# Taking the low part of five weight slabs from an adding transfer, on one Trainium2 core

## The chip, the cores and the metric

The kernel runs on one core of one Trainium2 chip. The metric is the device time of one execution in microseconds. The kernel before took 734.05 us, the median of three runs (733.32 to 734.15). All times inside the execution come from one profiled execution.

## What is computed

The reference is two blocks of a small transformer-like model on 256 tokens of width 1024, one after the other. The first block is a gated recurrent layer and an attention layer. The second block is a mixer and a feed-forward layer, then a pooling mixer and another feed-forward layer. The stretch around the change is the mixer of the second block:

```python
h = rmsnorm(x, norm_mix_g)
p = h @ w_in_ab                                   # 1024 -> 1536
ya = fnet_heads(p[..., :512], fnet_map)           # Fourier transform over tokens and channels, then a map
u = p[..., 512:1024] * sigmoid(p[..., 1024:])
u = conv31(u) + conv_b                            # a filter of 31 taps along the tokens, per channel
yb = silu(layernorm_per_head(u))
x = x + concat([ya, yb]) @ w_out_ab               # slabs 26 to 29
h = rmsnorm(x, norm_ffn_g)
x = x + (silu(h @ w_gate) * (h @ w_up)) @ w_down  # slabs 30, 31, 32, ...
```

## The kernel before

**Slabs.** The weights stream from HBM in slabs of 128 partitions by 2048 floats (1 MB). SyncE's queue loads each slab into one of five `raw` buffers (L597); before it loads a buffer again it waits until the slab in it has been used. There are 97 slabs that are multiplied in the split form below, numbered 0 to 96 (the list `MATS`).

**The split.** A product in the short float format (fp32r) loses bits, so each weight is written as a high and a low part, and each product is done three times: high by high, high by low and low by high (L1601, L1602 and L1603). Slab k has the tile `W[(k + 2) % 4]`, with the high part in `[:, 0]` and the low part in `[:, 1]`. ScalarE makes the high part, a copy of the raw slab into fp32r (the helper at L629, called in its `stream`), and counts it in `s_hi`. VectorE makes the low part, raw minus high (the helper at L1029, called in its own `stream`), and counts it in `s_lo`. TensorE waits for `s_lo` in `weights(k)`. SyncE frees the raw buffer on `s_lo` as well. ScalarE may overwrite a tile W only when TensorE has finished slab k - 4 (`before_split`).

**The order of work** is written out by hand, on each engine for itself. `fill(k)` on ScalarE and on VectorE splits all slabs up to k + 3 that are not yet split. So the place of a `fill` in an engine's list decides when a slab is split there. The calls that matter here are:

- `fill(24)` splits slabs 26 and 27, `fill(25)` slab 28, `fill(26)` slab 29, `fill(27)` slab 30, `fill(28)` slab 31.
- On ScalarE `fill(24)` stands before the copies of the outputs `a` 0 and 1 (to F2), and `fill(25)` before those of `a` 2 and 3. The products of L1872 read these copies. `fill(26)` stands between the root (L905) and the silu (L911) of the layer norm of head 3. `fill(27)` and `fill(28)` stand before two copies of the mixer's output into X, its squares (L943), and the high parts of the turned X (`turned_high`, L949).
- On VectorE `fill(24)` stands after 36 taps of the convolution (L1032), `fill(25)` after the low parts of the Fourier branch, `fill(26)` after the last taps, and `fill(27)` and `fill(28)` before the low parts of the turned X (`turned_low`, L1032).

Three of the four heads of the convolution are done on VectorE, one multiply-add of 128x256 per tap. Head 3 is done on TensorE (L1894), against diagonal matrices that ScalarE makes.

**TensorE** goes through: the products of slabs 22 to 25; the Fourier products (L1872, L1880, L1881, L1887); the convolution of head 3 (L1894); the residual (L1937); the products of slabs 26 to 29 (the function `mixed`), with the sums of the layer norm between them (L1900, L1905, L1661); then, in the feed-forward layer, turning X (L1927) and `gate_up`, which begins with slab 30. `mixed(7, 1)` is the first that needs slab 29, `mixed(7, 0)` the first that needs slab 28.

**GpSimd's queue** holds only four transfers: the Fourier matrix, then (after `s_flo` reaches 4) the matrix `rc` of the pooling and the row `prow`, then (after `s_cv3`) the row `frow`. `s_flo` counts the low parts of the Fourier branch, which VectorE makes.

Of the kernel before, what the change touches and what calls it, by code (L numbers as in the profile page):

```python
# [93 lines left out]
NRAW, NSPL, LOOK, NT, NB, NSQ = 5, 4, 3, 8, 8, 2  # L94
# [4 lines left out]
MATS = [i for i in RING if PLAN[i][0] not in ("first", "mod")]  # L99
# [11 lines left out]
def width(i):  # L111
    return PLAN[i][4] * 256 if PLAN[i][0] == "mat" else D if PLAN[i][0] == "u" else 2048
# [197 lines left out]

OUT = outputs()

ROWS_AT = {0: 1, 1: 2}
HALF_AT = {k: n + 1 for n, k in enumerate(k for k in range(len(MATS)) if OUT.end[k] is None)}

# [13 lines left out]
def two_block_program(nc, w_d, vec_d, cst_d, dft_d, rcnt_d, row_d, x_d, out_d):  # L329
# [3 lines left out]
    ADD, SUB, MUL = ALU.add, ALU.subtract, ALU.mult  # L333

    ctx = ExitStack()
    with ctx:
        def sb(name, shape, dt=f32):
            return ctx.enter_context(nc.sbuf_tensor(name, shape, dt))

        def sem(name):  # L340
            return ctx.enter_context(nc.semaphore(name))
# [7 lines left out]
        W = [sb(f"w{i}", [P, 2, 2048], f32r) for i in range(NSPL)]  # L349
# [36 lines left out]
            sem(f"s_{n}") for n in ("vec", "id", "xa", "xb", "cst", "dft", "rc", "prow", "frow", "out"))  # L386


        s_hi, s_lo, s_mod, s_half = (sem(f"s_{n}") for n in ("hi", "lo", "mod", "half"))

        s_ps = sem("s_ps")

# [30 lines left out]
        def V(name, i, n=1):  # L423
            return vec[:, VOFF[name] + i:VOFF[name] + i + n]
# [34 lines left out]
        def own_of(slab):  # L459
            return slab[0], slab[1] if slab[0] == "heads" else slab[3]  # L460

        def own(kind, at):

            n = next(n for n, i in enumerate(OWN) if own_of(PLAN[i]) == (kind, at))
            return own_at[kind, at], (s_own[n], 16)
# [4 lines left out]
        def out_of(*name):  # L470
            return PB[OUT.bank[name]][:, 0:T]
# [4 lines left out]
        def quarter(of, a, c):  # L476
            return of[:, a, c * 512:c * 512 + 512]
# [23 lines left out]
        def ended(*name):  # L501
            return s_ps, OUT.count[name]
# [4 lines left out]
        def landed(i):  # L507
            n = RING.index(i)
            return s_raw[n % NRAW], 16 * (n // NRAW + 1)

        def raw_of(i):
            return raw[RING.index(i) % NRAW]

        def before_split(k):

            return slab_ended(k - NSPL) if k >= NSPL else ended(*(("g", 3), ("g", 7), ("y", 3), ("y", 7))[k])
# [6 lines left out]
        def freed(name):  # L523
# [7 lines left out]
            if kind == "n":  # L531
                return s_rt, ROWS_AT[i]
            if kind == "ns":
# [43 lines left out]
        @block.sync  # L577
        def _(e):
            p = Port(e)
            e.dma_start(vec[:, :], vec_d).then_inc(s_vec, 16)  # L580
            e.dma_start(cst[:, 0:P], cst_d[:, 0:P]).then_inc(s_id, 16)
            e.dma_start(X[:, 0:4, :], x_d[:, 0:4, :]).then_inc(s_xa, 16)
            e.dma_start(X[:, 4:8, :], x_d[:, 4:8, :]).then_inc(s_xb, 16)
            n_mod = n_mat = 0
            emptied = []
            for i, slab in enumerate(PLAN):
                n = width(i)
                if i in OWN:
                    if slab[0] == "y":
                        p.wait_ge(*ended("u", 7))  # L590
                    place, done = own(*own_of(slab))
                    e.dma_start(place, w_d[i, :, 0:n]).then_inc(done[0], 16)
                    continue
                m = len(emptied)
                if m >= NRAW:
                    p.wait_ge(*emptied[m - NRAW])
                e.dma_start(raw[m % NRAW][:, 0:n], w_d[i, :, 0:n]).then_inc(s_raw[m % NRAW], 16)  # L597
                if slab[0] in ("first", "mod"):
                    n_mod += 1
                    emptied.append((s_mod, n_mod))  # L600
                else:
                    n_mat += 1
                    emptied.append((s_lo, n_mat))
                    if n_mat == 6:
                        e.dma_start(cst[:, P:NC], cst_d[:, P:NC]).then_inc(s_cst, 16)
            for a in range(2):
                p.wait_ge(s_fin0, a + 1)
                e.dma_start(out_d[:, a, 0:512], quarter(Of, a, 0)).then_inc(s_out, 16)
                p.wait_ge(s_fin1, a + 1)
                e.dma_start(out_d[:, a, 512:1024], quarter(Of, a, 1)).then_inc(s_out, 16)  # L610
            e.wait_ge(s_out, 16 * 4)

        @block.gpsimd
        def _(e):
            e.wait_ge(s_mv, 12)
            e.dma_start(acc[0][:, :], dft_d).then_inc(s_dft, 16)
            e.wait_ge(s_flo, 4)
            e.dma_start(rc, rcnt_d).then_inc(s_rc, 16)
            e.dma_start(prow[:, :], row_d[0]).then_inc(s_prow, 16)
            e.wait_ge(s_cv3, 1)  # L620
            e.dma_start(frow[:, :], row_d[1]).then_inc(s_frow, 16)

        @block.scalar
        def _(e):
            p = Port(e)
            at = {"plan": 0, "mat": 0}

            def copy(out, in_, **kw):
                return e.activation(out, in_, ACT.Copy, **kw)  # L629

            def stream(upto):

                while at["plan"] <= upto:
                    i = at["plan"]
                    at["plan"] += 1
                    if i not in MATS:
                        continue
                    k, n = at["mat"], width(i)
                    at["mat"] += 1
                    p.wait_ge(*landed(i))  # L640
                    p.wait_ge(*before_split(k))
                    copy(W[(k + 2) % NSPL][:, 0, 0:n], raw_of(i)[:, 0:n]).then_inc(s_hi, 1)

            def fill(k):
                stream(MATS[min(k + LOOK, len(MATS) - 1)])
# [18 lines left out]
            def row_root(i):  # L664
                p.wait_ge(*ended("n", i))
                if ROWS_AT[i] > 1:
                    p.wait_ge(s_rs, ROWS_AT[i] - 1)
                e.activation(root[:, :], out_of("n", i), ACT.Sqrt, scale=1.0 / D, bias=V("eps", 0)).then_inc(s_rt, 1)
# [44 lines left out]
            for q in range(2):  # L713
                half = F0f[:, 4 * q:4 * q + 4, :]
# [309 lines left out]
        def _(e):  # L1024
            p = Port(e)
            at = {"plan": 0, "mat": 0, "mod": 0, "vec": 1}

            def tt_(out, a, b, op):
                return e.tensor_tensor(out, a, b, op)  # L1029
# [11 lines left out]
            def mod_sum(i):  # L1041

                m, j = at["mod"], PLAN[i][4]
                u = UNIT_OF[PLAN[i][1:4]]
                at["mod"] += 1
                p.wait_ge(*landed(i))
                p.wait_ge(s_silu, 2)
                for q in range(2):
                    w, total = raw_of(i)[:, q * D:q * D + D], mv[:, u, 2 * j + q:2 * j + q + 1]
                    done = stt(w, w, 1.0, silu_c, MUL, MUL, accum_out=total)  # L1050
                done.then_inc(s_mod, 1)
                bias, off, name, goff = UNITS[u]
                if u in (5, 6):
                    two = mv[:, u, 2 * j:2 * j + 2]
                    p.wait_ge(s_mod, 8 + m + 1)
                    tt_(two, two, V(bias, off + 2 * j, 2), ADD).then_inc(s_mg if name else s_mq, 1)
                    if name:
                        p.wait_ge(s_mg, j + 1)
                        stt(two, two, 1.0, V(name, goff + 2 * j, 2), ADD, MUL).then_inc(s_mq, 1)
                elif j == 3:  # L1060
                    p.wait_ge(s_mod, 8 + m + 1)
                    tt_(mv[:, u, :], mv[:, u, :], V(bias, off, 8), ADD).then_inc(s_gain if name else s_mv, 1)
                    if name:
                        gain(u)

            def stream(upto):

                while at["plan"] <= upto:
                    i = at["plan"]
                    at["plan"] += 1  # L1070
                    if PLAN[i][0] == "mod":
                        mod_sum(i)
                    if i not in MATS:
                        continue
                    k, n = at["mat"], width(i)
                    at["mat"] += 1
                    w = W[(k + 2) % NSPL]
                    p.wait_ge(s_hi, k + 1)
                    tt_(w[:, 1, 0:n], raw_of(i)[:, 0:n], w[:, 0, 0:n].bitcast(f32), SUB).then_inc(s_lo, 1)
# [20 lines left out]
            def row_close(i):  # L1100
                p.wait_ge(s_rt, ROWS_AT[i])
                e.reciprocal(RS[i][:, :], root[:, :]).then_inc(s_rs, 1)
# [63 lines left out]
            z, y_, s_, s2, po = (sm[:, i, :] for i in (1, 3, 4, 5, 6))  # L1166
# [23 lines left out]
            for c in range(4):  # L1190
                for j in range(3):
                    for b in range(2):
                        d, n = 2 * c + b, 6 * c + 2 * j + b
# [398 lines left out]
        def _(e):  # L1592
            p = Port(e)
# [9 lines left out]
                return e.matmul(out, a_lo, b_hi, start=False, stop=stop)  # L1603

            def weights(k):
                p.wait_ge(s_lo, k + 1)

            def tile_of(k, half, o, R, r, out, start, stop, tok):
                w = W[(k + 2) % NSPL]
# [558 lines left out]
```

## Time and profile before

| | |
|---|---|
| median of the runs (lowest, highest) | 734.05 us (733.32, 734.15) |
| span of the profiled execution, first to last instruction | 731.6 us |
| TensorE, products | 719.8 us, 98% of the span |
| TensorE, weight loads | 629.7 us, 86% |
| VectorE | 502.8 us, 69% |
| ScalarE | 395.2 us, 54% |
| GpSimd | 2.4 us |
| mean traffic of the transfers | 213 GB/s |

The profiled execution's own time is not listed beside its span; the median of the runs is 2.45 us above the span. An engine's share says how much of the span it worked, not whether the end waited for it: products on TensorE overlap, and their ends are modelled. The timeline rows have the start in us, the time in us, the engine, the line and the operation, the tile written and the tiles read, the shapes, the count, and in brackets the idle time before it with what ended it.

### The profile page before, as it was taken

Reading aid. Unit: us, or ns where it says so; the run is one execution under the profiler, and the core shown is the slowest. Engines: PE = TensorE matmul, PEld = TensorE weight load, DVE = VectorE, ACT = ScalarE, POOL = GpSimd, SP = SyncE. Lnnn points to the kernel's source line nnn. Section 1 sums busy time; section 2 is a strip of 40 time slices with the busy share of each in tenths; the row PEclk is TensorE's granted clock in tenths of the full one; section 3 lists DMA queues with packets and bytes.
Section 4 is the critical chain, followed back from the end, with each engine's and each line's share of the span. In section 5 each row is a group of like instructions: output and inputs, shape, how many; then the busy total and the mean of one; then the engine's idle time right before and its main releaser. Section 6 shows DMA issues by size and latency. Waiting matters only on the chain.

```text
span 731.6 us, 9776 instructions
## 1 busy us (share of the span) xinstructions
PE 719.8 (98%) x3940; PEld 629.7 (86%) x3940; DVE 502.8 (69%) x801; ACT 395.2 (54%) x614; POOL 2.4 (0%) x8
## 2 busy tenths in 40 slices
PE   7999999999999999999999999999999999999996
PEld 6888889999999999888888888888888888888885
DVE  5879996998877889977744555555686445555544
ACT  3167446874886675658644434443666444344423
POOL 0000000000000000000000000000000000000000
PEclk9999999999999999999999999999999999999999
DMA  8999994798835343423755545554336555455201
GB/s 329 416 422 422 421 410 154 259 396 327 325 124 212 135 161 116 179 102 116 288 177 197 201 173 180 206 190 172 116 116 229 176 198 200 173 181 207 73 1 57
DMA packets 23085, 156.13 MB, mean 213 GB/s; under 512 B 2560, under 2 KB 2816, under 8 KB 5120
## 3 DMA queue, kind: packets, MB, share of 16 engines
q1 hardware_dynamic: 22464, 152.88, 55.2%
q0 software_dynamic: 576, 2.62, 0.9%
q8 instruction: 31, 0.51, 0.3%
q14 instruction: 14, 0.11, 0.0%
HBM read 154.44 MB, written 1.05 MB: 213 GB/s over the span
## 4 chain that ended last, share of the span: by engine, by line
PE 87%; DVE 6%; DMA 4%; ACT 2%; SPq 1%; issue 0%; ACTq 0%
PE pb L1601 22%; PE pb L1603 22%; PE pb L1602 21%; PE pb L1665 10%; DMA raw<-w_dram 4%; DVE raw L1032 3%; DVE w L1029 2%; PE pb L1894 2%; PE pb L2005 1%; PE pb L1758 1%; PE pb L1757 1%; PE pb L1759 1%; PE pb L2073 1%; PE pb L1927 1%; PE pb L1937 0%; PE pb L1872 0%
## 5 line engine op out<-in xcount | busy, mean ns | idle before, releaser
L1029 DVE TENSOR_TENSOR w<-raw,w 128x2048 fp32r<-128x2048 f32 x97 | 221.4, 2291 | 141.2 <-ACT w L629 141.2
L629 ACT ACTIVATE w<-raw 128x2048 fp32r<-128x2048 f32 x97 | 184.9, 1915 | 138.7 <-PE pb L1603 114.7
L1601 PE MATMUL pb<-w,r 128*128 128x512 f32 (+1 forms) x640 | 244.6, 382 | 0.0
L1603 PE MATMUL pb<-w,r 128*128 128x512 f32 (+1 forms) x640 | 241.1, 377 | 0.0
L1602 PE MATMUL pb<-w,r 128*128 128x512 f32 (+1 forms) x640 | 240.7, 376 | 0.0
L1603 PEld LDWEIGHTS pb<-w,r 128*128 128x128 f32 x640 | 120.4, 188 | 22.6
L1601 PEld LDWEIGHTS pb<-w,r 128*128 128x128 f32 x640 | 120.6, 188 | 21.2 <-issue 0.2
L1602 PEld LDWEIGHTS pb<-w,r 128*128 128x128 f32 x640 | 120.6, 188 | 21.0
L1601 PE MATMUL pb<-r,w 128*128 128x256 f32 x288 | 82.5, 287 | 0.4 <-DVE r L1029 0.4
L1603 PE MATMUL pb<-r,w 128*128 128x256 f32 x288 | 81.5, 283 | 0.0
L1602 PE MATMUL pb<-r,w 128*128 128x256 f32 x288 | 81.5, 283 | 0.0
L1032 DVE SCALAR_TENSOR_TENSOR raw<-raw,acc 128x1024 f32<-128x1024 f32 x64 | 75.1, 1221 | 5.0 <-DMA raw<-w_dram 5.0
L1665 PE MATMUL pb<-h,ow 128*128 128x256 f32 x256 | 57.0, 381 | 1.4 <-issue 0.6
L1665 PEld LDWEIGHTS pb<-h,ow 128*128 128x128 f32 x256 | 48.1, 190 | 10.1 <-issue 3.9
L1601 PEld LDWEIGHTS pb<-r,w 128*128 128x128 f32 x288 | 55.2, 192 | 0.6 <-issue 0.6
L1602 PEld LDWEIGHTS pb<-r,w 128*128 128x128 f32 x288 | 55.2, 192 | 0.1
L1603 PEld LDWEIGHTS pb<-r,w 128*128 128x128 f32 x288 | 55.2, 192 | 0.0
L963 ACT ACTIVATE t<-pb,rn 128x256 f32<-128x256 f32 x44 | 20.7, 476 | 59.6 <-PE pb L1603 59.6
L1032 DVE SCALAR_TENSOR_TENSOR f<-f,vec 128x256 f32<-128x256 f32 x114 | 46.7, 482 | 0.2
L1032 DVE SCALAR_TENSOR_TENSOR t<-pb,rn,t 128x256 f32<-128x256 f32 x44 | 21.1, 483 | 22.7 <-ACT t L963 22.7
L1665 PE MATMUL pb<-t,ow 128*128 128x256 f32 x128 | 27.8, 379 | 0.0
L1665 PEld LDWEIGHTS pb<-t,ow 128*128 128x128 f32 x128 | 24.3, 190 | 3.3
(208 smaller groups left out, 673.6 us busy)
## 6 DMA issues: line engine op xcount, KB each, us to landing
raw<-w_dram SPq DMA_DIRECT2D x129, 1024.0 KB, 4.9
ow<-w_dram SPq DMA_DIRECT2D x8, 1024.0 KB, 15.3
ow<-w_dram SPq DMA_DIRECT2D x8, 512.0 KB, 16.9
oh<-w_dram SPq DMA_DIRECT2D x2, 1024.0 KB, 22.5
x<-x_dram SPq DMA_DIRECT2D x2, 512.0 KB, 5.3
f<-rc_dram POOLq DMA_DIRECT2D x1, 1024.0 KB, 5.6
acc<-row_dram POOLq DMA_DIRECT2D x2, 512.0 KB, 6.7
out_dram<-f SPq DMA_DIRECT2D x4, 256.0 KB, 2.3
```

The costliest lines, as they stand in the source:

```text
L629: return e.activation(out, in_, ACT.Copy, **kw)
L963: e.activation(tt[(at_ - 1) % 4][:, :], bank_of("gu", layer, i, a)[:, 0:T], ACT.Silu, scale=rn[:, 2 * layer, a:a + 1]).then_inc(s_sgt, 1)
L1029: return e.tensor_tensor(out, a, b, op)
L1032: return e.scalar_tensor_tensor(out, a, s, b, op0, op1, **kw)
L1601: e.matmul(out, a_hi, b_hi, start=start, stop=False)
L1602: e.matmul(out, a_hi, b_lo, start=False, stop=False)
L1603: return e.matmul(out, a_lo, b_hi, start=False, stop=stop)
L1665: return e.matmul(out, slab[:, o:o + P], rhs, start=start, stop=stop)
L1757: e.matmul(with_shift, w[:, 0, o:o + P], raw_key(kt), start=kt == 0, stop=False)
L1758: e.matmul(with_shift, w[:, 1, o:o + P], raw_key(kt), start=False, stop=False)
L1759: done = e.matmul(out_of(*name), w[:, 0, o:o + P], lo_of(R2, kt), start=False, stop=kt == KT - 1)
L1894: done = e.matmul(out_of("cv", 3), dg[j % 8], G0[:, 3, j:j + T], start=j == 0, stop=j == 30)
```

## The change

For slabs 26 to 30, ScalarE writes minus the high part into `W[:, 1]` right after the high part, with a second copy of the raw slab (scale -1), and counts it in a new semaphore `s_minus`. GpSimd's queue waits for that and issues a transfer that reads the slab once more from HBM and adds it to `W[:, 1]`. TensorE waits for that transfer's own semaphore instead of `s_lo`. VectorE skips these five slabs. SyncE frees their raw buffers on `s_minus`.

```diff
+BY_DMA = [26, 27, 28, 29, 30]
+LOW_AT = {k: n + 1 for n, k in enumerate(k for k in range(len(MATS)) if k not in BY_DMA)}
...
-                    emptied.append((s_lo, n_mat))
+                    k = n_mat - 1
+                    emptied.append((s_minus, BY_DMA.index(k) + 1) if k in BY_DMA else (s_lo, LOW_AT[k]))
...
             e.wait_ge(s_mv, 12)
             e.dma_start(acc[0][:, :], dft_d).then_inc(s_dft, 16)
+
+            def low_sum(k):
+                e.wait_ge(s_minus, BY_DMA.index(k) + 1)
+                e.dma_start(W[(k + 2) % NSPL][:, 1, :], w_d[MATS[k]], accum_op=ADD).then_inc(s_sum[k], 16)
+
+            low_sum(26)
+            low_sum(27)
             e.wait_ge(s_flo, 4)
             e.dma_start(rc, rcnt_d).then_inc(s_rc, 16)
             e.dma_start(prow[:, :], row_d[0]).then_inc(s_prow, 16)
+            low_sum(28)
+            low_sum(29)
+            low_sum(30)
             e.wait_ge(s_cv3, 1)
             e.dma_start(frow[:, :], row_d[1]).then_inc(s_frow, 16)
...
                     copy(W[(k + 2) % NSPL][:, 0, 0:n], raw_of(i)[:, 0:n]).then_inc(s_hi, 1)
+                    if k in BY_DMA:
+                        copy(W[(k + 2) % NSPL][:, 1, 0:n], raw_of(i)[:, 0:n], scale=-1.0).then_inc(s_minus, 1)
...
                     at["mat"] += 1
+                    if k in BY_DMA:
+                        continue
                     w = W[(k + 2) % NSPL]
                     p.wait_ge(s_hi, k + 1)
                     tt_(w[:, 1, 0:n], raw_of(i)[:, 0:n], w[:, 0, 0:n].bitcast(f32), SUB).then_inc(s_lo, 1)
...
             def weights(k):
-                p.wait_ge(s_lo, k + 1)
+                if k in BY_DMA:
+                    p.wait_ge(s_sum[k], 16)
+                else:
+                    p.wait_ge(s_lo, LOW_AT[k])
```

## Rows read from the trace of the kernel before

**Rows 1.** The page: busy time, share of the span, instructions.
```profile
PE 719.8 (98%) x3940; PEld 629.7 (86%) x3940; DVE 502.8 (69%) x801; ACT 395.2 (54%) x614; POOL 2.4 (0%) x8
```
**Rows 2.** Windows: each engine's busy time (instructions), clock, transfers' share, GB/s.
```profile
260.00:310.00 50.00, 50.00 (x325) 46.83 (x325) 47.62 (x100) 32.61 (x67) 1.58 (x3) 1.00 0.38 145
310.00:340.00 30.00, 30.00 (x154) 25.03 (x153) 22.51 (x48) 20.11 (x36) 0.00 (x0) 1.00 0.35 130
340.00:400.00 60.00, 60.00 (x276) 49.70 (x275) 36.68 (x36) 34.05 (x39) 0.00 (x0) 1.00 0.55 201
```
**Rows 3.** Waits of TensorE: us in total, times, longest.
```profile
PE pb L1686 <- DVE f L1029: 2.0, 1, 2.0
...
PE pb L1601 <- DVE r L1029: 0.4, 1, 0.4
```
**Rows 4.** The page, costliest groups: the two passes of the split.
```profile
L1029 DVE TENSOR_TENSOR w<-raw,w 128x2048 fp32r<-128x2048 f32 x97 | 221.4, 2291 | 141.2 <-ACT w L629 141.2
L629 ACT ACTIVATE w<-raw 128x2048 fp32r<-128x2048 f32 x97 | 184.9, 1915 | 138.7 <-PE pb L1603 114.7
```
**Rows 5.** Timeline of VectorE at the first sum of head 3.
```profile
308.60 0.42 DVE L1032 SCALAR_TENSOR_TENSOR f<-pb,f 128x256 f32<-128x256 f32 x1 [0.82 <-PE pb L1900]
```
**Rows 6.** Timeline of ScalarE and TensorE around slabs 26 to 28.
```profile
270.66 3.71 ACT L629 ACTIVATE w<-raw 128x2048 fp32r<-128x2048 f32 x2
...
280.90 0.39 ACT L629 ACTIVATE f<-pb 128x256 f32<-128x256 f32 x1 [2.50 <-PE pb L1603]
...
280.70 3.62 PE L1872 MATMUL pb<-cst,f 128*128 128x256 f32 x16
```
**Rows 7.** Timeline of all engines around slab 29, 313 to 322 us.
```profile
313.66 1.90 ACT L629 ACTIVATE w<-raw 128x2048 fp32r<-128x2048 f32 x1
...
317.33 0.51 ACT L911 ACTIVATE t<-f,vec 128x256 f32<-128x256 f32 x1 [0.47 <-DVE f L1032]
317.87 0.42 ACT L629 ACTIVATE r<-t 128x256 fp32r<-128x256 f32 x1
319.17 0.42 DVE L1029 TENSOR_TENSOR r<-t,r 128x256 fp32r<-128x256 f32 x1
...
319.51 2.04 DVE L1032 SCALAR_TENSOR_TENSOR f<-f,vec 128x256 f32<-128x256 f32 x4
...
321.63 0.68 PE L1900 MATMUL pb<-f,ones_sb 128*128 128x256 f32 x2
```
**Rows 8.** Timeline around slabs 30 and 31; first use of 29 and 30.
```profile
329.99 3.71 ACT L629 ACTIVATE w<-raw 128x2048 fp32r<-128x2048 f32 x2
333.60 0.58 ACT L629 ACTIVATE x<-pb 128x512 f32<-128x512 f32 x1
334.69 0.60 ACT L629 ACTIVATE x<-pb 128x512 f32<-128x512 f32 x1 [0.51 <-PE pb L1603]
...
336.49 2.18 ACT L949 ACTIVATE r<-pb,vec 128x128 fp32r<-128x128 f32 x8
...
337.67 2.16 DVE L1032 SCALAR_TENSOR_TENSOR r<-pb,vec,r 128x128 fp32r<-128x128 f32 x8 [0.97 <-ACT r L949]
...
327.52 0.48 PE L1601 MATMUL pb<-w,r 128*128 128x512 f32 x1
...
338.12 0.47 PE L1601 MATMUL pb<-w,r 128*128 128x512 f32 x1
```
**Rows 9.** Transfers: issue on GpSimd's queue, issues with KB and us to landing.
```profile
303.51 0.53 POOL L618 DMA_DIRECT2D f<-rc_dram  x1 [118.25 <-DVE r L1029]
...
raw<-w_dram SPq DMA_DIRECT2D x129, 1024.0 KB, 4.9
...
f<-rc_dram POOLq DMA_DIRECT2D x1, 1024.0 KB, 5.6
...
acc<-dft_dram POOLq DMA_DIRECT2D x1, 512.0 KB, 9.4
```
**Rows 10.** A window in which the transfers are saturated; columns as in Rows 2.
```profile
50.00:90.00 40.00, 40.00 (x187) 35.20 (x186) 39.20 (x78) 23.37 (x45) 0.00 (x0) 1.00 1.01 420
```

More of the change, by code:

```diff
@@ L386, in two_block_program @@
             sem(f"s_{n}") for n in ("vec", "id", "xa", "xb", "cst", "dft", "rc", "prow", "frow", "out"))
-        s_hi, s_lo, s_mod, s_half = (sem(f"s_{n}") for n in ("hi", "lo", "mod", "half"))
+        s_hi, s_lo, s_mod, s_half, s_minus = (sem(f"s_{n}") for n in ("hi", "lo", "mod", "half", "minus"))
+        s_sum = {k: sem(f"s_sum{k}") for k in BY_DMA}
         s_ps = sem("s_ps")
```

## Prediction

> **What bounds the kernel now.** I read the page's busy times first: products fill 719.8 of the 731.6 us [rows 1]. A busy TensorE alone proves little, so I then read the windows by stage: in the stretch of the change, and behind it, TensorE is busy in every microsecond at full clock, while VectorE has 47.62 of 50 us from 260 to 310 and only 22.51 of 30 from 310 to 340 [rows 2]. Third, the waits of TensorE: the largest is 2.0 us near the start, and from 60 to 255 us there are three, of which 0.4 us is the longest; from 255 us to the end the view lists none [rows 3]. So TensorE sets the time from the change's stretch to the end, with nothing lost that a freed VectorE could give back. Two consequences: relief elsewhere is worth almost nothing, and each microsecond in which TensorE must wait for one of the five slabs is lost for good, since no later wait exists that could absorb it.
>
> The sum is made in the trace's times (span 731.6 us) and its difference is put on the median of the runs, 734.05 us, which is 2.45 us above the span.
>
> **What is removed.** Five VectorE passes of 2.29 us, 11.5 us [rows 4]. VectorE gets to the low parts of the Fourier branch 4.4 us earlier (slabs 26, 27) and ends them with 2.3 us more in hand (slab 28), but its next step is the centring of head 3 at 308.60, which already now waits 0.82 us for a product of TensorE [rows 5]. The lead ends in that wait. The passes of slabs 29 and 30 stand ahead of steps that wait for ScalarE or TensorE too: `turned_low` idled 0.97 us for ScalarE's high parts [rows 8]. I cost the relief at nothing; its cover is that wait. Below nothing (a gain) it can reach only if TensorE waits for VectorE inside its modelled busy time, a rival below.
>
> **What is added on ScalarE.** Five copies of 1.915 us [rows 4]. Two in a row take 3.71 us [rows 6], so an inserted one moves what follows by 3.71 - 1.91 = 1.80 us.
>
> - Slabs 26 to 28: three copies, 5.4 us. The two high parts begin at 270.66; the next work was the copies of `a` 0 and 1, the high part of slab 28, and the copies of `a` 2 and 3, of which the last started at 280.90 after an idle 2.50 us [rows 6]. Laid out again: 26 and 27 end at 277.9, `a` 0 and 1 by 278.5, slab 28 with its negative by 282.1, and `a` 2 is there at 282.5. The products of L1872 start at 280.70, and four heads share 3.5 us, so the third head begins at 282.6, when its copy is just there. Cost 0.1 us, between 0 and 0.4.
> - Slab 29: one copy, from 315.46 to 317.4. Then the table load of 1.28 us (the function table must be loaded again before the silu) moves to 317.4 to 318.7, and the silu from 317.33 to 318.7; the high part of head 3, which began at 317.87, ends at 319.66 instead of 318.3. VectorE wants it at 319.17, and behind it stand the last four taps (2.04 us), and behind these the mean product of TensorE at 321.63 [rows 7]. That product already follows the taps' end (319.51 + 2.04 = 321.55) within a tenth. So 0.5 us reach TensorE. Between 0.3 and 0.7.
> - Slab 30: one copy ahead of slab 31 and of the copies into X. The first X copy moves from 333.60 to 335.4, the second from 334.69 to 335.9; squares, high parts and low parts follow. The high parts begin 1.2 us later than 336.49, the low parts 1.2 us later than 337.67, and the first product of `gate_up` at 338.12 needs the first of these low parts, which lands only some 0.2 us before it [rows 8]. So by this chain `gate_up` begins 1.2 us late, whatever the transfer does.
>
> **What is added on GpSimd's queue, and TensorE's new wait.** The queue is empty but for three transfers, with issue slots of 0.53 us [rows 9]. Slabs 26 and 27 are ready to be added at 274.3 and 277.9 and needed from 310.1 on; slab 28 stands behind `rc` and `prow`, which wait for VectorE's Fourier low parts (now about 299), and is needed at about 325. These three are hidden. `frow`, queued behind slab 30, is needed only at the end. Slab 29: negative ready at 317.4, needed at 327.52 [rows 8], 10.1 us. Slab 30: negative ready at 329.99 + 1.80 + 1.91 = 333.7, needed at 338.12: only 4.4 us [rows 8]. Behind TensorE's wait for slab 30 stands all of the feed-forward layer.
>
> How long does an adding transfer take? No row shows one. A plain 1 MB transfer of this queue took 5.6 us, one of SyncE's queue 4.9 us in the median [rows 9]. At saturation 420 GB/s flow [rows 10], so 1.05 MB are 2.5 us of it, and 3.1 us of the 5.6 are start and end. The addition must read the tile too: 3.1 + 2 x 2.5 = 8.1 us. The raw buffer of slab 30 is freed in the same moment as the addition is released, so the load of slab 35 runs beside it; sharing all of it would give 10.6 us. I take 9.0. Ends: 4.9 us (no dearer than a load) and 18.8 us (twice the 9.4 us that half a megabyte once took on this queue in a crowded stretch [rows 9]). The queue's own start after a release takes 0.3 us (low part done at 303.2, issue at 303.51 [rows 9]).
>
> The Trainium skill (Collectives: The Full Stack, "The bandwidth ceiling: the fold count and why AG ≠ RS ≠ AR") says that an add in the transfer engines costs no time for the adding, but reads two sources through one read ring, and so moves at about half a copy's pace; its DMA: Bandwidth & Descriptors ("Anatomy of one DMA — SWDGE (gpsimd) path") gives 2.0 us plus the bytes at 436 GB/s. Estimated from these two pages, 2.1 MB take 6.8 us, which would put the whole change at +3.3 us, 737.4 us, still within the case I forecast. No run shown so far has such an add.
>
> **Sum.** Slab 30 holds TensorE 0.3 + 9.0 - 4.4 = 4.9 us, and the 1.2 us of ScalarE's chain lie inside it. Slab 29 (9.3 against 10.1 us) is just hidden. Total 0.1 + 0.5 + 4.9 = 5.5 us: 734.05 + 5.5 = 739.6 us.
>
> **The rivals.**
> - *The adding transfer is as quick as a load.* At 4.9 to 6.5 us to landing, slab 30 holds 0.8 to 2.4 us, so ScalarE's 1.2 us or a little more decide: +1.8 to +3.0 us, 736.4 us. For it: the transfers are idle two thirds of this stretch (share 0.35 [rows 2]). Against it: the second read, and the load of slab 35 beside it.
> - *The adding transfer is far slower.* From 10.1 us on slab 29 holds TensorE too, but its wait lies ahead of slab 30's and inside it. At 12 to 18.8 us: 0.6 + 0.3 + (12 to 18.8) - 4.4 = +8.5 to +15.3 us, 746 us in the middle. For it: the 9.4 us for half a megabyte. Against it: that was in a crowded stretch.
> - *VectorE is the true limit of the convolution (not slower, or faster).* The ends of products are modelled, so a wait could lie hidden in the busy time. Place: 286 to 323 us. Then slab 28's 2.3 us and slab 29's 2.2 us come back, and with a transfer as quick as a load 734.05 + 1.8 - 4.5 = 731.4 us. It decides from the point where VectorE no longer idles ahead of 308.60. Against it: it does idle there, 0.82 us, and TensorE's list has no wait [rows 3, 5]. With half of it, and all transfers hidden, the time is the old one.
> - *The low part is not what it was.* The sum need not be rounded to the short format as VectorE's was. This would change bits and not the time, so it has no chance of its own.
>
> **How the numbers follow.** Chances: the forecast (stall 3.0 to 7.5 us in all) 0.47, the quick transfer 0.26, the slow one 0.16, VectorE as the limit or all hidden 0.11. A kernel of this spread tells a change from none at about 0.2%, 1.5 us. Slower by more than that: 0.47 + 0.16 + 0.23 of the quick case = 0.86; the rest of the quick case and 0.07 of the last make 0.10 for the same; 0.04 for faster. The range takes in the quick case from +1.4 us and the slow one up to +12: 735.4 to 746.0 us.
>
> **What would show it.** Right: a wait of TensorE at L1601 at `gate_up`'s start, around 339 to 343 us, ended by an addition of GpSimd's queue into w, of 4 to 6 us; landing of these transfers near 9 us; the silu of head 3 about 1.3 us later and the mean product at L1900 half a microsecond late; no wait anywhere before 282 us; TensorE gapless from slab 31 to the end; VectorE idle some 8 us ahead of the centring of head 3. Wrong: additions that land within 5 us, a wait at slab 26 or 28, or a stretch from 280 to 340 us that is shorter than before.

## The result and the profile after

The changed kernel takes 744.12 us, the median of four runs (743.33 to 744.99), against 733.69 us for the kernel before (the median of four runs, one more than ahead of the prediction). The ratio is 1.0139, with a 95% interval of [1.0125, 1.0152], so it is 10.2 us slower (9.2 to 11.2). The span of the profiled execution went from 731.6 to 741.5 us. The page after, where it answers to [rows 1] and to the two split passes of [rows 4]:

```profile
PE 722.7 (97%) x3940; PEld 632.1 (85%) x3940; DVE 491.7 (66%) x796; ACT 402.9 (54%) x619; POOL 7.0 (1%) x13
...
L1046 DVE TENSOR_TENSOR w<-raw,w 128x2048 fp32r<-128x2048 f32 x92 | 210.0, 2290 | 144.8 <-ACT w L644 144.8
L644 ACT ACTIVATE w<-raw 128x2048 fp32r<-128x2048 f32 x102 | 193.8, 1913 | 138.6 <-PE pb L1622 114.7
...
w<-w_dram POOLq DMA_DIRECT2D x5, 1024.0 KB, 12.0
```

The work moved as described: five passes fewer on VectorE (92 instead of 97), five more on ScalarE (102), five transfers on GpSimd's queue. Their median time to landing is 12.0 us. Lines have shifted: L1601 is now L1620, L1900 is L1922, L1937 is L1959, L1927 is L1949.

The waits of TensorE after, where [rows 3] had none behind 255 us (total, times, longest):

```profile
PE pb L1620 <- DMA w<-w_dram: 6.9, 1, 6.9
PE pb L1708 <- DVE f L1046: 3.2, 1, 3.2
...
PE pb L1922 <- DVE f L1049: 0.3, 1, 0.3
```

The first is the new one: a single wait of 6.9 us for an adding transfer. The third is new too, at the mean product behind the last taps. The second is the start-up wait, which lies at 2.0 us in [rows 3] and varies from run to run (1.9 to 3.8 us in the traces here); here it moved nothing, since the products at 317.77 us stand at the same time in both traces. The list leaves out waits under 0.15 us and those that the modelled end of the product before covers.

Timeline after of TensorE, GpSimd's queue and SyncE's queue, from the release of slab 30 to the products behind it:

```profile
334.21 0.33 SPq L601 DMA_DIRECT2D raw<-w_dram  x1
...
334.48 0.86 POOL L625 DMA_DIRECT2D w<-w_dram  x1 [15.96 <-ACT w L644]
335.02 0.89 POOL L636 DMA_DIRECT2D acc<-row_dram  x1
...
338.34 0.33 SPq L601 DMA_DIRECT2D raw<-w_dram  x1
...
345.99 0.80 PE L1620 MATMUL pb<-w,r 128*128 128x512 f32 x1 [6.89 <-DMA w<-w_dram]
346.59 0.63 PE L1621 MATMUL pb<-w,r 128*128 128x512 f32 x1
347.01 0.63 PE L1622 MATMUL pb<-w,r 128*128 128x512 f32 x1
...
350.64 0.39 PE L1622 MATMUL pb<-w,r 128*128 128x512 f32 x1
```

Beside the addition (issued at 334.48) are issued the loads of slabs 35 (334.21) and 36 (338.34), and frow's transfer (335.02). The first product of `gate_up` starts at 345.99, where [rows 8] have it at 338.12: 7.9 us lost. Then the starts of products are 0.427 us apart instead of 0.23, ten of them until 350.41: another 2.0 us. Together they are the 9.9 us by which the span grew. The windows show what the slow products are (busy time with counts, clock, transfers' share, GB/s):

```profile
345.99:350.41 4.42, 4.42 (x10) 3.48 (x11) 0.00 (x0) 0.00 (x0) 0.00 (x0) 0.50 0.40 167
351.00:355.40 4.40, 4.40 (x26) 3.76 (x25) 2.16 (x8) 3.89 (x9) 0.00 (x0) 1.00 0.00 0
```

Behind the idle 6.9 us TensorE was granted 0.50 of its clock, the lower level of 1.2 GHz, for the first 4.4 us of products, and 1.00 (2.4 GHz) afterwards.

### The profile page after: what moved, and what is told of

It reads as the page before. It is cut to its first block, busy times and chain, and to the rows that moved or that the text cites. A ratio compares the mean times of both kernels' runs of the same rounds, so it can differ in the third digit from the quotient of the medians.

```text
span 741.5 us, 9781 instructions
## 1 busy us (share of the span) xinstructions
PE 722.7 (97%) x3940; PEld 632.1 (85%) x3940; DVE 491.7 (66%) x796; ACT 402.9 (54%) x619; POOL 7.0 (1%) x13
## 3 DMA queue, kind: packets, MB, share of 16 engines
HBM read 159.69 MB, written 1.05 MB: 217 GB/s over the span
## 4 chain that ended last, share of the span: by engine, by line
PE 87%; DVE 6%; ACT 3%; DMA 2%; issue 0%; SPq 0%; DVEq 0%; ACTq 0%
PE pb L1620 21%; PE pb L1622 21%; PE pb L1621 21%; PE pb L1687 13%; DVE raw L1049 2%; DVE w L1046 2%; PE pb L1916 2%; DMA w<-w_dram 2%; PE pb L2027 1%; ACT w L644 1%; PE pb L1780 1%; PE pb L1779 1%; PE pb L1781 1%; PE pb L2095 1%; DMA x<-x_dram 1%; PE pb L1949 1%
## 5 line engine op out<-in xcount | busy, mean ns | idle before, releaser
L1046 DVE TENSOR_TENSOR w<-raw,w 128x2048 fp32r<-128x2048 f32 x92 | 210.0, 2290 | 144.8 <-ACT w L644 144.8
L644 ACT ACTIVATE w<-raw 128x2048 fp32r<-128x2048 f32 x102 | 193.8, 1913 | 138.6 <-PE pb L1622 114.7
L1620 PE MATMUL pb<-w,r 128*128 128x512 f32 (+1 forms) x640 | 245.6, 384 | 6.9 <-DMA w<-w_dram 6.9
L1620 PEld LDWEIGHTS pb<-w,r 128*128 128x128 f32 x640 | 121.1, 189 | 28.4 <-DMA w<-w_dram 7.3
L1620 PE MATMUL pb<-r,w 128*128 128x256 f32 x288 | 82.5, 287 | 0.4 <-DVE r L1046 0.4
L1620 PEld LDWEIGHTS pb<-r,w 128*128 128x128 f32 x288 | 55.2, 192 | 0.6 <-issue 0.6
## 6 DMA issues: line engine op xcount, KB each, us to landing
ow<-w_dram SPq DMA_DIRECT2D x8, 1024.0 KB, 15.3
acc<-row_dram POOLq DMA_DIRECT2D x2, 512.0 KB, 10.2
```

The source lines that it names most:

```text
L1620: e.matmul(out, a_hi, b_hi, start=start, stop=False)
```

## The experiments

Each ratio is against the kernel before on the same chip, and a difference in us is worked out from the ratios unless two medians stand beside it. Where the list of slabs is shorter, the `low_sum` calls of the slabs left out are gone too. The diffs show the main lines.

**Slabs 26, 27 and 28 alone.**
```diff
-BY_DMA = [26, 27, 28, 29, 30]
+BY_DMA = [26, 27, 28]
```


> Only slabs 26, 27 and 28 get their low part from the adding transfer; 29 and 30 go by VectorE as before. Theory (TensorE sets the time; only slabs 29 and 30 cost, through ScalarE's order and the landing): no wait of TensorE is added, 0.0 to +0.4 us against before. Rival (VectorE's relief is worth something in the convolution): -1 to -2.3 us. Rival (the traffic or the copies slow all of the stretch): +1 us or more.

Measured: 733.59 against 733.58 us, ratio 1.0001 [0.9992, 1.0009]. TensorE has no wait behind 255 us. These transfers land in 13.5, 17.4 and 11.6 us, longer than slab 30's, and no product waits for them. Three ScalarE copies, 3 MB more of traffic and three VectorE passes saved come to nothing together; since VectorE's relief alone brings nothing (below), the copies and the traffic cost nothing that the time shows.

**Slab 30 alone.**
```diff
-BY_DMA = [26, 27, 28, 29, 30]
+BY_DMA = [30]
```


> Only slab 30 goes by the adding transfer. Theory: nearly the whole loss is here: TensorE's first product of gate_up waits till about 345.5 us (338.1 before), and some ten products behind it run at the lower clock; +8.5 to +10 us against before. Rival (the loss is shared out over slabs 26 to 30, or slab 29 holds TensorE): under +6 us.

Measured: 743.44 us, ratio 1.0128 [1.0113, 1.0144], +9.4 us. Landing in 11.5 us, and in its list of waits the same line as in the full change:

```profile
PE pb L1616 <- DMA w<-w_dram: 6.9, 1, 6.9
```

One slab of the five carries about nine tenths of the loss.

**Slabs 26 to 29.**
```diff
-BY_DMA = [26, 27, 28, 29, 30]
+BY_DMA = [26, 27, 28, 29]
```


> Slabs 26 to 29 by the adding transfer, slab 30 by VectorE. Theory: slab 29's transfer (10.4 us) lands just before TensorE wants it, so only the delay of head 3's high part by ScalarE is paid: +0.3 to +0.7 us against before, with a wait of about 0.3 us at the mean product behind the last taps. Rival (slab 29's transfer holds TensorE): +1 us or more, with a wait at the first product of slab 29.

Measured: 734.02 us against 733.48, ratio 1.0008 [0.9999, 1.0016]. The interval just touches one, so the time alone doesn't show slab 29's term. The trace does. It has the wait of 0.3 us, and lists none for a transfer, though slab 29's took 10.4 us to land:

```profile
PE pb L1921 <- DVE f L1048: 0.3, 1, 0.3
```

Slab 29's transfer was not quite free, though, and the starts show it. The first line is of the kernel before, the other two of the changed kernel; the last is the first product of slab 29, and the others are the small products ahead of it:

```profile
326.26 1.50 PE L1661 MATMUL pb<-cst,lnr 128*128 128x128 f32 x12
```
```profile
326.75 1.50 PE L1683 MATMUL pb<-cst,lnr 128*128 128x128 f32 x12
328.08 0.50 PE L1620 MATMUL pb<-w,r 128*128 128x512 f32 x1
```

Before, the product at 327.52 [rows 8] came 1.26 us after 326.26. In the changed kernel it came 1.33 us after 326.75, right behind the landing at 328.04 (317.66 + 10.38); in this kernel 1.38 us after, right behind the landing at 328.30. Where slab 29 landed at 325.5 us (minus first, below) it was 1.26 us again. So the wait for slab 29 took about 0.1 us, too little for the list, and nothing was left to spare.

**The negated copies without the transfers.** The kernel before with the five negated copies; VectorE waits for the negative and writes the low part over it.
```diff
+                    if k in BY_DMA:
+                        copy(W[(k + 2) % NSPL][:, 1, 0:n], raw_of(i)[:, 0:n], scale=-1.0).then_inc(s_minus, 1)
...
+                    if k in BY_DMA:
+                        p.wait_ge(s_minus, BY_DMA.index(k) + 1)
                     tt_(w[:, 1, 0:n], raw_of(i)[:, 0:n], w[:, 0, 0:n].bitcast(f32), SUB).then_inc(s_lo, 1)
```


> ScalarE makes the five negated copies, but VectorE then makes the low parts over them as before, so no adding transfer runs. Theory: only the moves of ScalarE's order remain: 0.3 to 0.7 us at the mean product behind the last taps and 1.2 us at the start of gate_up, +1.7 us in all, between +1.2 and +2.3. Rival (the copies are hidden, all is the transfer): under +0.4 us. Rival (the copies cost most of the loss): over +4 us.

Measured: 735.31 us, ratio 1.0020 [1.0012, 1.0029], +1.5 us. Its two new waits of TensorE behind 255 us are 0.3 us at the mean product and this one at the start of `gate_up`:

```profile
340.09 0.47 PE L1607 MATMUL pb<-w,r 128*128 128x512 f32 x1 [0.59 <-issue]
```

The profile names no releaser for it, but VectorE's low parts of the turned X, which this product reads, start at 339.64 where they started at 337.67 (2.0 us later, as the product is). So ScalarE's order is a real cost of its own, 1.5 us. In the full change most of it lies inside the 6.9 us wait.

**VectorE's relief alone.** The kernel before without the low parts of slabs 26 to 30; TensorE then waits for the high part alone and multiplies by what lies in the low part's place, and SyncE frees the raw buffer on the high part.
```diff
+                    if k in LEFT:
+                        continue
                     w = W[(k + 2) % NSPL]
                     p.wait_ge(s_hi, k + 1)
```


> The kernel before with VectorE's low parts of slabs 26 to 30 left out (TensorE multiplies by what lies there): VectorE's relief alone, 11.5 us of it, with nothing added. Theory: TensorE waits for VectorE nowhere, so 0.0 us, between -0.3 and +0.2. Rival (VectorE is the true limit of the convolution): -2 to -4.5 us.

Measured: 733.46 against 733.58 us, ratio 1.0000 [0.9991, 1.0008]. Taking 11.5 us off VectorE is worth nothing, and the timeline shows where they go. VectorE now waits 7.4 us ahead of the centring of head 3, where [rows 5] have 0.82:

```profile
308.26 0.42 DVE L1036 SCALAR_TENSOR_TENSOR f<-pb,f 128x256 f32<-128x256 f32 x1 [7.43 <-PE pb L1906]
```

**Idle products in the wait for slab 30.**
```diff
+                if layer == 0 and i == 0 and kts[0] == 0 and halves[0] == 0:
+                    bank_free("gu", layer, i, 0)
+                    for _ in range(16):
+                        e.matmul(bank_of("gu", layer, i, 0)[:, 0:T], ones, sqt[0][:, :], start=True, stop=True)
```


> The changed kernel, with 16 idle products of 128x256 (0.43 us each, 6.9 us together) ahead of TensorE's wait for slab 30, into the bank that gate_up then starts afresh. Theory (the idle wait of 6.9 us brings the lower clock, and ten products then take 0.43 instead of 0.23 us): the granted clock stays at its upper level, 1.5 to 2.0 us faster than the changed kernel. Rival (the slow products have another cause, such as the transfers' writes into the tile): the same time, and slow products at the same place.

Measured: 742.03 us, ratio 1.0111 [1.0094, 1.0128]. That is 8.1 us above before, where the changed kernel was 10.2 above it, so about 2 us less. The two intervals still touch; against the kernel with only frow moved (below), which took 744.54 us on the same chip, it is 2.5 us less, and there they don't. The windows of the idle products and of the twelve products behind them:

```profile
340.00:347.10 7.10, 7.09 (x33) 5.89 (x31) 3.51 (x11) 2.64 (x10) 0.00 (x0) 1.00 0.99 257
347.15:350.00 2.85, 2.85 (x12) 2.31 (x13) 0.00 (x0) 0.00 (x0) 0.00 (x0) 1.00 0.63 262
```

The clock stays at 1.00, though the same transfers run and slab 30's lands in 11.5 us again. The slow products came from the idle wait, not from the transfers.

**The transfers as plain copies.** The low part is then the whole weight.
```diff
-                e.dma_start(W[(k + 2) % NSPL][:, 1, :], w_d[MATS[k]], accum_op=ADD).then_inc(s_sum[k], 16)
+                e.dma_start(W[(k + 2) % NSPL][:, 1, :], w_d[MATS[k]]).then_inc(s_sum[k], 16)
```


> The changed kernel with the five transfers as plain copies on the same queue, without the addition (the low part is then the whole weight, so the output is another). Theory (the second read makes the transfer slow): slab 30 lands in 6 to 7.5 us instead of 11.5, and the time is +3 to +5 us against before, without the lower clock or with less of it. Rival (the queue or what runs beside it makes it slow): landing still 10 us or more, time within 1.5 us of the changed kernel.

Measured: 738.49 us, ratio 1.0061 [1.0046, 1.0076], +4.5 us. Slab 30 lands in 7.0 us instead of 11.5 under the same neighbours, so the addition costs 4.5 us of landing. The lower clock did not stay away. It came here behind a wait of 2.5 us, from the third product on (the last line is a window as above, with 0.57 of the clock in the mean):

```profile
341.93 0.50 PE L1620 MATMUL pb<-w,r 128*128 128x512 f32 x1 [2.46 <-DMA w<-w_dram]
342.27 0.50 PE L1621 MATMUL pb<-w,r 128*128 128x512 f32 x1
342.56 0.63 PE L1622 MATMUL pb<-w,r 128*128 128x512 f32 x1
...
341.90:345.60 3.70, 3.67 (x10) 2.85 (x11) 1.22 (x3) 1.34 (x4) 0.00 (x0) 0.57 0.86 354
```

**frow moved ahead of slab 29.**
```diff
             low_sum(28)
+            e.wait_ge(s_cv3, 1)
+            e.dma_start(frow[:, :], row_d[1]).then_inc(s_frow, 16)
             low_sum(29)
             low_sum(30)
-            e.wait_ge(s_cv3, 1)
-            e.dma_start(frow[:, :], row_d[1]).then_inc(s_frow, 16)
```


> The changed kernel with the transfer of frow (0.5 MB) issued ahead of slab 29's, at about 307 us, instead of right behind slab 30's. Theory (frow shares the engines with slab 30's addition): slab 30 lands about 1 us sooner, in 10 to 10.8 us, as slab 29's did in 10.4; -0.7 to -1.3 us against the changed kernel. Rival (a transfer queued behind doesn't slow the one ahead): no change.

Measured: 744.54 us, ratio 1.0148 [1.0133, 1.0164]. My theory missed. Slab 30 still lands in 11.7 us, and TensorE waits 7.1 us. A transfer queued behind this one on its own queue doesn't slow it. The packets in the trace of the changed kernel say why: frow's first one moves at 345.47, after the addition's last.

**The addition alone.** As the last one, and the load of slab 35 is held as well, and with it that of slab 36 behind it in SyncE's order.
```diff
-                    emptied.append((s_minus, BY_DMA.index(k) + 1) if k in BY_DMA else (s_lo, LOW_AT[k]))
+                    emptied.append((s_sum[k], 16) if k == 30 else (s_minus, BY_DMA.index(k) + 1) if k in BY_DMA else (s_lo, LOW_AT[k]))
```


> As the kernel with frow moved, and SyncE also holds the load of slab 35 (and all behind it) until slab 30's addition has landed, so that the addition runs alone. Theory (its own cost is two reads, 3.1 + 2 x 2.5 us by the rows of before): lands in 8 to 9 us, -2.5 to -3.5 us against the changed kernel, more if the clock recovers sooner. Rival (the addition is slow by itself): lands in 10 us or more.

Measured: 741.21 us, ratio 1.0101 [1.0086, 1.0116], 3.3 us below the kernel with only frow moved. What the trace says of slab 30's transfer, first with the two loads beside it (the changed kernel; 11.7 us and a wait of 7.1 with frow moved) and then alone (this one):

```profile
  PE pb L1620: 6.9, 1
busy tenths in 40 slices 0000000000000000000000000000000000000000
DMA to landing us min/median/max: 11.5/11.5/11.5
```
```profile
  PE pb L1620: 3.6, 1
busy tenths in 40 slices 0000000000000000000000000000000000000000
DMA to landing us min/median/max: 8.2/8.2/8.2
```

Alone it lands in 8.2 us, where the reckoning with two reads had 8.1. The windows from the issue to the first packet of the addition show what the loads do (columns as above), in the changed kernel and then in this one:

```profile
334.48:338.82 4.34, 4.28 (x24) 3.23 (x22) 2.36 (x2) 4.34 (x11) 1.42 (x2) 1.00 0.84 242
```
```profile
334.97:336.56 1.59, 1.59 (x9) 1.32 (x8) 0.05 (x1) 1.59 (x2) 0.87 (x1) 1.00 0.00 0
```

In the first, 242 GB/s in 4.34 us are 1.05 MB, which is the load of slab 35, issued 0.27 us ahead of the addition. The addition's own packets start only when that load is nearly through, 4.3 us after the issue; alone they start after 1.6 us. Slab 29's addition, with one load ahead of it (slab 34), also started after 4.3 us and landed in 10.4. So of the 3.3 us some 2.2 go to the load ahead and 1.1 to the load of slab 36, which joins at 342.05. That is read from the traces; no kernel was run that holds only one of the two loads. Twelve products still run at the lower clock.

**The addition alone, with idle products.** Nine of them, where the expectation says eight.
```diff
+                if layer == 0 and i == 0 and kts[0] == 0 and halves[0] == 0:
+                    bank_free("gu", layer, i, 0)
+                    for _ in range(9):
+                        e.matmul(bank_of("gu", layer, i, 0)[:, 0:T], ones, sqt[0][:, :], start=True, stop=True)
```


> The kernel in which slab 30's addition runs alone (landing 8.2 us), with 8 idle products of 128x256 (3.4 us together) in TensorE's wait. Theory (the 3.6 us of waiting bring the lower clock for twelve products): the slow products go, -2.0 to -2.5 us against the kernel without the idle products, about +5.2 us against before. Rival (they don't come from the idle wait): same time.

Measured: 738.62 us, ratio 1.0069 [1.0054, 1.0085], +5.1 us against before and 2.3 us less than without them. The twelve products behind the wait take 2.8 us instead of 5.3, at 1.00 instead of 0.50 of the clock:

```profile
342.90:345.70 2.80, 2.80 (x13) 2.26 (x13) 0.16 (x1) 0.50 (x2) 0.00 (x0) 1.00 0.66 196
```

**Minus first.** The negative is made ahead of the high part, TensorE waits for both, and the raw buffer is freed after both.
```diff
-                    copy(W[(k + 2) % NSPL][:, 0, 0:n], raw_of(i)[:, 0:n]).then_inc(s_hi, 1)
                     if k in BY_DMA:
                         copy(W[(k + 2) % NSPL][:, 1, 0:n], raw_of(i)[:, 0:n], scale=-1.0).then_inc(s_minus, 1)
+                    copy(W[(k + 2) % NSPL][:, 0, 0:n], raw_of(i)[:, 0:n]).then_inc(s_hi, 1)
```


> The changed kernel with ScalarE's two copies in the other order: first minus the high part, which releases the addition, then the high part (TensorE waits for both, SyncE frees the raw buffer after both). Theory (the landing of slab 30 sets the time, counted from its release): the addition starts 1.8 us sooner, and the load of slab 35 now starts 1.8 us behind it; -1.8 to -2.8 us against the changed kernel. Rival (the landing is fixed by the traffic's end, which doesn't move): under 0.8 us faster.

Measured: 739.44 us, ratio 1.0080 [1.0066, 1.0094], about 4.3 us below the changed kernel. That is in the theory's direction and past its numbers:

```profile
332.97 0.86 POOL L625 DMA_DIRECT2D w<-w_dram  x1 [15.95 <-ACT w L644]
...
342.26 0.76 PE L1620 MATMUL pb<-w,r 128*128 128x512 f32 x1 [2.87 <-DMA w<-w_dram]
```

Issued 1.5 us sooner than 334.48, it also lands in 9.2 instead of 11.5 us, 3.8 us sooner in all, and the first product comes 3.7 us sooner. The load of slab 35 is now issued behind it (334.50), and the places are exchanged: the addition's first packet moves 1.6 us after its issue, as it does alone, the load's 4.2 us after its own, and the load lands in 10.2 us instead of 5.5. I had left the second part out.

**Minus first, alone, frow ahead.** All three edits together.

> The copies in the other order, frow moved ahead and slab 35's load held until the addition has landed. Theory: release at 332.3, landing 0.3 + 8.2 us later at 340.8, against 339.7 when ScalarE's chain lets gate_up begin: a wait of some 2 us in all and little or no lower clock; +2.4 to +4 us against before. Rival (another wait shows up once the landing is short): over +5 us.

Measured: 736.32 us, ratio 1.0036 [1.0023, 1.0050], +2.6 us. The wait is short, and the clock stays up (1.00 from 341.20 to 344.00):

```profile
341.21 0.47 PE L1622 MATMUL pb<-w,r 128*128 128x512 f32 x1 [1.68 <-DMA w<-w_dram]
341.51 0.39 PE L1623 MATMUL pb<-w,r 128*128 128x512 f32 x1
```

This is the best form found that still has slab 30, and it is still slower than before. No form beat the kernel before, and with a relief that alone is worth nothing none of this kind is to be expected to.

## Why the prediction was right, and where it was short

- *TensorE sets the time, and the relief is worth nothing:* right. Relief alone gave 1.0000, slabs 26 to 28 gave 1.0001. VectorE idles 7.5 us ahead of the centring of head 3 in the changed kernel, where some 8 were foretold. The rival that VectorE limits the convolution fell.
- *The first three slabs are hidden, on ScalarE and in the queue:* right, with no listed wait before 319 us. The 0.1 us at the Fourier products is there too: from the first of them to the next line's it takes 3.54 us (280.61 to 284.15) where it took 3.46 (280.70 to 284.16). The working put the third head at 282.6, where its own rows give 280.70 + 1.75 = 282.45; the cost stays the same. Their landings, 12.0 to 16.4 us in the changed kernel, were well beyond what I allowed; the 25 us and more between release and need covered them.
- *0.5 us at the mean product:* right. The high part of head 3 moved to 319.21, VectorE waited for it, and TensorE waited 0.3 us. The product itself starts 0.47 us later, at 322.10 instead of 321.63 [rows 7].
- *1.2 us from ScalarE's chain at the start of `gate_up`:* right in kind. With the term before it, it was to make 1.7 us, and the negated copies alone gave 1.5.
- *Slab 29 just hidden:* true to 0.1 us, and by luck. A landing of 9.0 us left 0.8 us to spare; it took 10.4, which used that up and held TensorE for about 0.1 us. In the kernel with frow moved it took 10.6, and the first product of slab 29 came 1.54 us after the sums instead of 1.26, 0.3 us late.
- *Slab 30 holds TensorE 4.9 us, by a landing of 9.0 us:* right mechanism, mis-sized term. I had 8.1 us for the addition alone, and 8.2 was measured. For the load of slab 35 beside it I allowed 0.9 us, though sharing all of it would have given 10.6, and the load of slab 36, released by slab 31's low part, I left out. The two cost 3.3 us. I took the load beside the addition as sharing with it; in the trace it goes ahead of it, and the addition's packets start 4.3 us after the issue. The release came at 334.2 (0.5 us later, with TensorE's own delay), the issue at 334.48, the landing 11.5 us later. That moved the first product by 7.9 us in place of 5.5 for the whole change.
- *The clock:* not in the prediction at all. I costed a wait of TensorE at its length. Behind it come ten products at the lower level, 2.0 us. Idle products in the wait take these 2.0 us away.
- *frow:* rightly costed at nothing. It now goes right behind slab 30's addition, and moving it changed nothing.

Sum as measured: 7.9 (of it 0.5 from the mean product) + 2.0 = 9.9 us in the trace, 10.2 us by the ratio. The forecast was 5.5. Of the 4.4 us between it and the trace, 2.4 are the landing and 2.0 the clock.

That the time lies in the range is in part luck. The case I forecast had a delay of up to 7.5 us; the first product came 7.9 us late. The whole, +10.2 us, is a figure of the rival with the slow transfer (+8.5 to +15.3 us), whose landing of 12 us and more did not come either. It got there by the 2.0 us of clock, which no case held. The upper end was wide enough because it took in that rival, not because I had these two terms.

The Trainium skill (Collectives: The Full Stack, "The bandwidth ceiling: the fold count and why AG ≠ RS ≠ AR") says of an add between cores that it moves at about half a copy's pace because it reads two sources. The runs agree in the pace: the packets of 8 KB took 0.63 us each in the additions (the median) and 0.31 to 0.33 in plain transfers, and alone the addition landed 2.6 us later than the queue's plain transfer of 5.6 us [rows 9], where a second read of 1.05 MB at the saturated rate of [rows 10] would be 2.5. Beside the same loads the two are 4.5 us apart (11.5 and 7.0): the loads cost the addition 3.3 us and the plain transfer 1.4. Why they cost it more was not tried. With two pages' figures I had put the landing at 6.8 us; even alone it was 8.2.

## What to carry to other kernels

When the bounding engine has no waits, work moved off another engine buys nothing. What decides is the tightest gap between release and need on the new path: four of five slabs had 10 us and more and cost about 0.6 us, the one with 4.4 us cost nine. Time an addition in a transfer by what is issued just ahead of it, and release it before the next load, not together with it. To a new wait of TensorE add the products that run at the lower clock behind it (1.5 to 2.5 us here, behind waits of 2.5 us and more).

## What the runs showed of the hardware that was not expected

- An adding transfer of 1 MB landed in 8.2 us alone, 9.2 with loads issued 1.5 us and more behind it, 10.4 with one load issued just ahead, 11.5 with a second one behind, and 17.4 behind another addition and loads. Its packets took 0.63 us each against 0.31 of a plain transfer.
- Of two transfers on two queues the one issued first began to move first. Behind a load issued 0.27 us earlier, the addition's first packet came 4.3 us after its issue instead of 1.6. Behind an addition issued 1.5 us earlier, the load's came 4.2 us after its issue instead of 1.0.
- A transfer of 0.5 MB issued right behind on the same queue didn't slow it (11.5 and 11.7 us).
- After TensorE had been idle for 6.9, 3.6, 2.9 and 2.5 us, seven to twelve products of 128x512 ran at 0.43 instead of 0.23 us. After 1.7 us none did.
